# mLSTM scan: 20 thrown-away products of 512 columns at its opening are given up

## The chip, the cores and the metric

The kernel runs on one core of one Trainium2 chip. The metric is the device time of that core in microseconds (us), from launch to end. A core has TensorE for matrix products (PE in the profile, with its weight loads as a row of their own, PEld), VectorE (DVE), ScalarE (ACT), GpSimd (POOL) and SyncE (SP); they run beside one another and wait for one another through semaphores.

## The reference

Two layers of a diffusion backbone work on 1024 latent tokens and 256 context tokens of width 1024. Each layer projects its tokens once and hands the columns to four mixers: differential attention, a bidirectional mLSTM, a bidirectional gated linear attention (GLA) and windowed attention. A gate, one output projection and a residual follow. The part that bears on the change is the mLSTM, run forward and backward over the tokens in chunks, with a state (`cmat`, `nvec`, `m`) that is carried from chunk to chunk:

```
def _mlstm_step(state, xs):
    cmat, nvec, m = state
    q, k, v, li, lf = xs
    b = jnp.cumsum(lf, axis=-1)
    d = jnp.where(tril, b[..., :, None] - b[..., None, :] + li[..., None, :], -jnp.inf)
    m_t = jnp.maximum(m_inter, jnp.max(d, axis=-1))
    w = jnp.exp(d - m_t[..., None])
    s = jnp.einsum('bhtd,bhsd->bhts', q, k) * w
    num = jnp.einsum('bhts,bhsv->bhtv', s, v) + g_inter[..., None] * jnp.einsum('bhvd,bhtd->bhtv', cmat, q)
    nq = jnp.sum(s, axis=-1) + g_inter * jnp.einsum('bhd,bhtd->bht', nvec, q)
    h = num / jnp.maximum(jnp.abs(nq), jnp.exp(-m_t))[..., None]
    cmat = decay[..., None, None] * cmat + jnp.einsum('bhs,bhsv,bhsd->bhvd', w_end, v, k)
```

## The kernel before, in words

The program is a row of stages, run for each of the two layers; a stage is a block in which every engine has its own instruction list, and the engines meet at the end of a block. In `stage_mlstm` a first block (line 845) projects the tokens, convolves and gates them, turns them (line 949) and prepares decays. The second block (line 1128) is the scan, and it is the one the change touches. The GLA stage, whose block opens at line 1460, comes right behind it.

The scan works on chunks of 128 tokens: 10 chunks by two directions, 20 units in the list `UNITS`, forward and backward in turn. For one unit TensorE issues five groups, four heads each:

- `logs(u)`: the exponents of the weights, as one product of 128x512 that lays down the mask (line 1207, from the tiles `same`, an identity, and `neg`, the mask) and four of 128x128 that add the rows of gate sums (line 1210, from `row_parts` and `sel`). It writes PSUM bank `u % 2`.
- `scores(u)`: q times k of the four heads (line 1218).
- the new state's share, keys by scaled values (line 1238), and the share of the old state (line 1241).
- the weighted scores by the values (line 1248).

TensorE runs ahead by one unit: its list is logs(0), scores(0), and then for each u: logs(u+1), lines 1238 and 1241 of u, scores(u+1), line 1248 of u. ScalarE takes the exponential of each head's logs (line 1258). VectorE multiplies it with the scores (`weigh`, line 1277) and combines the parts into state and result (`finish`, lines 1285 to 1301). GpSimd divides and scales the values (lines 1173 to 1187).

At the opening, GpSimd copies `neg` and `same` (lines 1166 and 1167, signal `parts`), and VectorE copies and splits the gate sums into `row_parts` and copies `sel` (lines 1263, 1264 and 1267, signal `lows`, three increments). `logs(0)` waits for both signals. Ahead of it TensorE's list holds a loop of `WARM = 20` products of 128x512 on `same` and `neg` (lines 1222 to 1225), which waits for `parts` alone and writes PSUM bank 1. Nothing reads what it writes there; logs(1) later writes that bank anew.

Of the kernel before, what the change touches and what calls it, by code (L numbers as in the profile page):

```python
# [23 lines left out]
P = 128  # L24
# [9 lines left out]
HEADS = 4  # L34
# [69 lines left out]
def layer_program(nc, dram):  # L104

    ctx = ExitStack()
    with ctx:
# [37 lines left out]
        for layer in range(DEPTH):  # L145
            env["layer"], env["last"] = layer, layer == DEPTH - 1
            for stage in (stage_entry, stage_mlstm, stage_gla, stage_diff_attention,
                          stage_window_attention, stage_gates, stage_output):
                with ExitStack() as own:
                    stage_ctx.append(own)  # L150
                    stage(nc, env)

                    nc.all_engine_barrier(sems_to_clear=range(first_free, first_free + len(stage_sems)))
                    if stage is stage_output:
                        nc.all_engine_barrier(sems_to_clear=range(loaded[0].sem.num, slab_used.sem.num + 1))
                stage_sems.clear()
# [653 lines left out]
def stage_mlstm(nc, env):  # L810
    ps, signal, yT, ring = (env[n] for n in ("ps", "signal", "yT", "ring"))
    outer = ExitStack()
    with outer:
# [31 lines left out]
        with ExitStack() as own, nc.Block() as block:  # L845
# [8 lines left out]
            @block.sync  # L854
            def _(sp):
                for n in range(2 * PARTS):
                    i, ks = n // PARTS, slice(n % PARTS * KT // PARTS, (n % PARTS + 1) * KT // PARTS)
                    proj.wait_used(sp, n)
                    at = SLAB_AT[S_MG + i]
                    src = env["dram"]["w"][env["layer"] * P:(env["layer"] + 1) * P, at + ks.start * 512:at + ks.stop * 512]  # L860
                    sp.dma_start(mod_w[:, i, ks, :].rearrange("p k n -> p (k n)"), src).then_inc(env["loaded"][S_MG + i].sem, 16)
                def move_rows():
                    sp.wait_ge(v_ones.sem, 4)
                    sp.wait_ge(lanes_ready.sem, 1)
                    for way in range(2):
                        for t in range(NT):
                            sp.dma_start(row_b[32 * way:32 * way + HEADS, t * P:(t + 1) * P],
                                         g_cm[64 * way + HEADS * t:64 * way + HEADS * (t + 1), :]).then_inc(row_moved.sem, 16)

                proj.release(sp, 1)  # L870
                for part in range(PARTS):
                    proj.wait_used(sp, 2 * KT + 2 * part)
                    load_part(sp, env, S_CV, part)
                move_rows()
                proj.release(sp, 3)
                load_slabs(sp, env, S_CQK, S_CQK + 1)
                sp.wait_ge(row_moved.sem, 2 * NT * 16)
# [250 lines left out]
        with ExitStack() as own, nc.Block() as block:  # L1128
            def tile(name, shape, dt=F32):
                return own.enter_context(env["sbuf"](name, shape, dt))  # L1130
# [3 lines left out]
            neg = tile("b_neg", [P, 2, P], F32R)  # L1134
            same = tile("b_same", [P, P], F32R)
# [5 lines left out]
            num = tile("b_num", [P, 2, HEADS, DH + 1])  # L1141
            den = tile("b_den", [P, 2, HEADS])
            NU = len(UNITS)
            WARM = 20

            def col(j, q, way):
                return cols[:, q, 64 * way + HEADS * j:64 * way + HEADS * (j + 1)]
# [1 line left out]
            def span(u):  # L1149
                return slice(UNITS[u][2] * P, (UNITS[u][2] + 1) * P)  # L1150

            def half(h):
                return slice(64 * (h % 2), 64 * (h % 2) + 64)

            def fresh_of(u, hp=slice(0, 2)):
                return ps[:, 4 + 2 * (u % 2), 2 * (DH + 1):4 * (DH + 1)].rearrange("p (a d) -> p a d", a=2)[:, hp, :]

            def intra_of(u):
                return ps[:, 5 + 2 * (u % 2), 2 * (DH + 1):6 * (DH + 1)].rearrange("p (h d) -> p h d", h=HEADS)

            def inter_of(u):
                return ps[:, 4 + 2 * (u % 2):6 + 2 * (u % 2), 0:2 * (DH + 1)].rearrange("p o (e d) -> p e o d", e=2)
# [34 lines left out]
            @block.tensor  # L1197
            def _(pe):
                def logs(u):
                    way, i, j = UNITS[u]  # L1200
                    if u == 0:
                        pe.wait_ge(parts.sem, 2)
                        pe.wait_ge(lows.sem, 3)
                    if u >= 2:
                        pe.wait_ge(w_ready.sem, HEADS * (u - 1))
                    bank = ps[:, u % 2, :]
                    pe.matmul(bank.rearrange("p (h t) -> p h t", h=HEADS), same[:, :],
                              neg[:, way, :].unsqueeze(1).broadcast_to([P, HEADS, P]), start=True, stop=False, skip_group_check=True)
                    for h in range(HEADS):
                        last = pe.matmul(bank[:, h * P:(h + 1) * P], sel[:, way * HEADS + h, :], row_parts[:, span(u)],  # L1210
                                         start=False, stop=h == HEADS - 1, skip_group_check=True)
                    last.then_inc(d_mm.sem, 1)

                def scores(u):
                    if u >= 1:
                        pe.wait_ge(sw_ready.sem, u)
                    for h in range(HEADS):
                        last = pe.matmul(ps[:, 2 + h % 2, h // 2 * P:(h // 2 + 1) * P], qkT[half(h), 2 + h // 2, span(u)],
                                         qkT[half(h), h // 2, span(u)], start=True, stop=True, tile_position=(64 * (h % 2), 0))
                    last.then_inc(s_mm.sem, 1)  # L1220

                pe.wait_ge(parts.sem, 2)
                for i in range(WARM):
                    pe.matmul(ps[:, 1, :].rearrange("p (h t) -> p h t", h=HEADS), same[:, :],
                              neg[:, 0, :].unsqueeze(1).broadcast_to([P, HEADS, P]), start=True, stop=True)
                logs(0)
                scores(0)
                for u, (way, i, j) in enumerate(UNITS):
                    if u + 1 < NU:
                        logs(u + 1)  # L1230
                    if u == 0:
                        pe.wait_ge(zeroed.sem, 1)
                    if u >= 2:
                        pe.wait_ge(state_ready.sem, 2 * (u - 1))
                        pe.wait_ge(num_ready.sem, u - 1)
                    pe.wait_ge(vw_ready.sem, u + 1)
                    for h in range(HEADS):
                        last = pe.matmul(fresh_of(u)[half(h), h // 2, :], ktm[:, j, h * DH:(h + 1) * DH],
                                         vw[:, u % 2, h, :], start=True, stop=True)
                    for h in range(HEADS):  # L1240
                        last = pe.matmul(inter_of(u)[:, h // 2, h % 2, :], qkT[half(h), h // 2, span(u)],
                                         state[half(h), way, h // 2, :], start=True, stop=True, tile_position=(64 * (h % 2), 0))
                    last.then_inc(u_mm.sem, 1)
                    if u + 1 < NU:
                        scores(u + 1)
                    pe.wait_ge(sw_ready.sem, u + 1)
                    for h in range(HEADS):
                        last = pe.matmul(intra_of(u)[:, h, :], sw[:, h, :], v1[:, j, h, :], start=True, stop=True)
                    last.then_inc(intra_mm.sem, 1)
# [186 lines left out]
def stage_gla(nc, env):  # L1436
# [3 lines left out]
    with outer:  # L1440
# [19 lines left out]
        with ExitStack() as own, nc.Block() as block:  # L1460
# [4 lines left out]
            BANKS = 6  # L1465
            WARM = 8
            NP = NT // 2
# [29 lines left out]
            def _(pe):  # L1497
# [51 lines left out]
                pe.wait_ge(first_decays.sem, 1)  # L1549
                for _ in range(WARM):  # L1550
                    pe.matmul(ps[:, 0, :], la_hi[:, 0, 0:P], la_hi[:, 0:2, :].rearrange("p t c -> p (t c)"), start=True, stop=True)
# [1438 lines left out]
```

## Time and profile before

| | us |
|---|---|
| median of 3 runs | 2335.21 |
| lowest and highest run | 2332.82 and 2339.88 |
| the profiled execution | 2340.97 |
| its span, first to last instruction | 2339.2 |
| PE busy in the span | 1982.7 (85%) |
| mean granted clock of TensorE | 0.929 |

[...] Times in the trace count from the first instruction. A matmul's own duration is longer than the distance to the next one, since they are pipelined; how fast TensorE works is read from the distance between starts. In a row of the timeline the bracket at the end tells how long the engine had been idle and who released it.

### The profile page before, as it was taken

The page shows a single profiled execution, that of the slowest core. Times are in us where ns is not written, and L with a number is a line of the kernel's source. Part 1 is how long each engine was busy: PE and PEld are TensorE (multiplying, and loading weights), DVE is VectorE, ACT ScalarE, POOL GpSimd, SP SyncE. Part 2 cuts the span into 40 slices and gives each one's busy share as a digit, 9 for nine tenths or more (in the row PEclk, how much of TensorE's full clock was granted, in tenths as well). Part 3 has the DMA queues.
Part 4 walks back from the last instruction along what each step waited for, and adds up shares of the span by engine and source line. Part 5 has one row for each costly group of instructions (what it writes and reads, how often), then busy time and mean ns, then how long its engine had stood idle before and what let it go on. Part 6 is the DMA issues. An engine that isn't in the chain of part 4 may idle for free. (4 is left out here: it accounts for less than half of the span.)

```text
span 2339.2 us, 37578 instructions
## 1 busy us (share of the span) xinstructions
PE 1982.7 (85%) x14664; PEld 1644.9 (70%) x14664; DVE 1354.3 (58%) x2545; ACT 985.9 (42%) x2076; POOL 500.5 (21%) x642
## 2 busy tenths in 40 slices
PE   5889889897777868898987988988987778688988
PEld 3778778786665647787866877877876566577767
DVE  5156428778878367222765356268578782672257
ACT  5243332336868436311224333322358684262121
POOL 2203325311010100322214124244120101002212
PEclk8899999998989979999998999998989898799999
DMA  9840350240000410313239601600420004102231
GB/s 397 294 139 2 96 158 2 58 124 1 1 1 1 140 41 1 91 58 125 113 124 337 197 27 46 182 27 5 116 62 1 1 1 131 49 2 72 72 127 54
DMA packets 69614, 203.25 MB, mean 87 GB/s; under 512 B 8096, under 2 KB 11456, under 8 KB 65984
## 3 DMA queue, kind: packets, MB, share of 16 engines
q0 software_dynamic: 38016, 93.34, 14.0%
q1 hardware_dynamic: 26240, 98.08, 11.6%
q10 hardware_dynamic: 5184, 9.44, 1.1%
q8 instruction: 118, 1.93, 0.3%
q14 instruction: 56, 0.46, 0.1%
HBM read 180.83 MB, written 19.92 MB: 86 GB/s over the span
## 5 line engine op out<-in xcount | busy, mean ns | idle before, releaser
L774 PE MATMUL ps<-ring_lo,h_hi 128*128 128x512 f32 (+3 forms) x800 | 271.5, 340 | 0.0
L774 PE MATMUL ps<-h_hi,ring_lo 128*128 128x512 f32 (+1 forms) x688 | 251.0, 365 | 0.0
L2375 DVE TENSOR_REDUCE a_st<-ps 128x1 f32<-128x1280 f32 (+1 forms) x144 | 196.7, 1369 | 42.7 <-PE ps L2260 42.2
L2328 ACT ACTIVATE ring<-ps,a_st 128x1280 f32<-128x1280 f32 (+1 forms) x144 | 177.4, 1232 | 54.7 <-DVE a_st L2375 54.4
L2260 PE MATMUL ps<-a_k,a_q 128*128 128x512 f32 (+1 forms) x400 | 126.7, 427 | 53.1 <-ACT ring L2328 48.7
L774 PEld LDWEIGHTS ps<-ring_lo,h_hi 128*128 128x128 f32 x800 | 158.7, 198 | 13.6 <-issue 0.5
L774 PE MATMUL ps<-h_hi,g_proj_wh 128*128 128x512 f32 (+1 forms) x400 | 148.9, 372 | 12.1 <-DVE ring_lo L732 7.2
L774 PE MATMUL ps<-g_proj_xl,g_proj_wh 128*128 128x512 f32 (+1 forms) x400 | 148.3, 371 | 0.0
L774 PEld LDWEIGHTS ps<-h_hi,ring_lo 128*128 128x128 f32 x688 | 130.3, 189 | 21.3
L2277 PE MATMUL ps<-cst,ring 128*128 128x128 f32 x656 | 107.2, 296 | 42.2 <-ACT ring L2337 16.3
L2260 PEld LDWEIGHTS ps<-a_k,a_q 128*128 128x128 f32 x400 | 73.8, 213 | 82.0 <-ACT ring L2328 65.7
L2753 PE MATMUL ps<-o_w_hi,o_y_hi 128*128 128x512 f32 x288 | 113.8, 395 | 17.1 <-DVE o_y_lo L2788 8.8
L2277 PEld LDWEIGHTS ps<-cst,ring 128*128 128x128 f32 x656 | 79.6, 150 | 63.9 <-ACT ring L2337 20.7
L774 PE MATMUL ps<-a_proj_wh,h_hi 128*128 128x512 f32 (+1 forms) x320 | 111.6, 349 | 7.0 <-DVE ring_lo L732 7.0
L2754 PE MATMUL ps<-o_w_lo,o_y_hi 128*128 128x512 f32 x288 | 113.3, 393 | 0.0
L2755 PE MATMUL ps<-o_w_hi,o_y_lo 128*128 128x512 f32 x288 | 113.3, 393 | 0.0
L2816 ACT ACTIVATE o_y_hi<-yT 128x640 fp32r<-128x640 f32 (+1 forms) x64 | 43.5, 686 | 152.7 <-PE ps L2755 144.3
L774 PE MATMUL ps<-a_proj_wh,a_proj_xl 128*128 128x512 f32 (+1 forms) x320 | 104.7, 336 | 0.0
L2665 DVE TENSOR_TENSOR par<-ps,par 128x512 f32<-128x512 f32 (+1 forms) x40 | 25.3, 636 | 136.9 <-ACT par L2647 136.9
L2647 ACT ACTIVATE par<-ps 128x512 f32<-128x512 f32 (+1 forms) x50 | 27.7, 554 | 180.7 <-PE ps L774 159.0
L2395 DVE SCALAR_TENSOR_TENSOR ring<-ring,a_st 128x1280 f32<-128x1280 f32 (+1 forms) x72 | 102.6, 1425 | 0.1
L2682 POOL TENSOR_TENSOR yT<-yT,par 128x512 f32<-128x512 f32 (+1 forms) x50 | 61.2, 1238 | 179.2 <-DVE par L2665 153.5
(379 smaller groups left out, 5258.5 us busy)
## 6 DMA issues: line engine op xcount, KB each, us to landing
ring<-in_w SPq DMA_DIRECT2D x14, 2048.0 KB, 7.5
a_proj_xl<-h_low POOLq DMA_DIRECT2D x64, 320.0 KB, 3.2
ring<-in_w SPq DMA_DIRECT2D x32, 512.0 KB, 3.8
b_proj_xl<-h_low POOLq DMA_DIRECT2D x22, 640.0 KB, 4.4
d_proj_xl<-h_low POOLq DMA_DIRECT2D x32, 320.0 KB, 3.2
h_low<-h_low SPq DMA_DIRECT2D x32, 256.0 KB, 4.1
yT<-in_w SPq DMA_DIRECT2D x16, 512.0 KB, 7.2
g_proj_xl<-h_low POOLq DMA_DIRECT2D x32, 256.0 KB, 5.5
```

What stands on the lines that cost most here:

```text
L774: last = pe.matmul(out, left, right, start=k == 0 and (p, q) == self.HIGH[0], stop=k == KT - 1 and (p, q) == self.LOW[0])
L2260: last = pe.matmul(ps[:, 3 * c + b, 0:w], q4[:, 2 * h + c, t * P:(t + 1) * P], k4[:, 2 * h + c, k0:k0 + w], start=True, stop=True)
L2277: last = pe.transpose(ps[:, 6 + n % 2, (k - a) * P:(k - a + 1) * P], p(u, 0, T)[:, k * P:(k + 1) * P], C(env, "ident"))
L2328: act.activation(p(u, c, n), ps[:, 3 * c:3 * c + 3, :].rearrange("p b n -> p (b n)")[:, 0:n], ACT.Exp, bias=st[:, 0:1], accum_out=st[:, 1: ...
L2375: dve.tensor_reduce(stat[:, u % SLOTS, c, 0:1], ps[:, 3 * c:3 * c + 3, :].rearrange("p b n -> p (b n)")[:, 0:n], AX.X, ALU.max, negate=Tru ...
L2395: dve.scalar_tensor_tensor(out=p(u, 0, n), in0=p(u, 1, n), scalar=st[:, 0, 3:4], in1=p(u, 0, n), op0=ALU.mult, op1=ALU.add).then_inc(comb. ...
L2647: act.activation(sig[:, n % 2, 0:w], ps[:, n % 8, 0:w], ACT.Sigmoid).then_inc(sg.sem, 1)
L2682: pool.tensor_tensor(y, y, sig[:, n % 2, 0:b[1]], ALU.mult).then_inc(done.sem, 1)
L2753: pe.matmul(ps[:, n % 8, :], y_hi[:, at, tile], w_hi[:, at, :], start=k == 0, stop=False)
L2754: pe.matmul(ps[:, n % 8, :], y_hi[:, at, tile], w_lo[:, at, :], start=False, stop=False)
L2755: last = pe.matmul(ps[:, n % 8, :], y_lo[:, at, tile], w_hi[:, at, :], start=False, stop=k == KT - 1)
L2816: act.activation(y_hi[:, i % BUFS, 0:HT], yT[:, k, toks(half)], ACT.Copy).then_inc(split_hi.sem, 1)
```

## The change

The loop of 20 products and its own wait for `parts` go out of TensorE's list, and with them the constant. `logs(0)` keeps both of its waits. Nothing else is touched. The lines behind move up by one, and those behind the loop by five.

```diff
@@ -1141,7 +1141,6 @@
             den = tile("b_den", [P, 2, HEADS])
             NU = len(UNITS)
-            WARM = 20
 
             def col(j, q, way):
@@ -1219,10 +1218,6 @@
                     last.then_inc(s_mm.sem, 1)
 
-                pe.wait_ge(parts.sem, 2)
-                for i in range(WARM):
-                    pe.matmul(ps[:, 1, :].rearrange("p (h t) -> p h t", h=HEADS), same[:, :],
-                              neg[:, 0, :].unsqueeze(1).broadcast_to([P, HEADS, P]), start=True, stop=True)
                 logs(0)
                 scores(0)
```

TensorE's list at the opening of the scan's block, before (`b_neg` and `b_same` are the tiles `neg` and `same`, `xN` stands for N in a row):

```order
536 L845 UNCONDITIONAL_BRANCH
537 L1197 UNCONDITIONAL_BRANCH
538 L1224 MATMUL ps<-b_neg,b_same 128x512 x20
539 L1207 MATMUL ps<-b_neg,b_same 128x512
540 L1210 MATMUL ps<-b_row_parts,b_sel 128x128 x4
541 L1218 MATMUL ps<-b_qkT 128x128 x4
542 L1207 MATMUL ps<-b_neg,b_same 128x512
```

The same place on TensorE with the change:

```order
536 L845 UNCONDITIONAL_BRANCH
537 L1196 UNCONDITIONAL_BRANCH
538 L1206 MATMUL ps<-b_neg,b_same 128x512
539 L1209 MATMUL ps<-b_row_parts,b_sel 128x128 x4
540 L1217 MATMUL ps<-b_qkT 128x128 x4
541 L1206 MATMUL ps<-b_neg,b_same 128x512
```

The group of 20 is gone, and logs(0) is the first thing TensorE does in the block. The order of all that follows is the same, in both layers, and so are the lists of the other engines.

## Rows read from the trace of the kernel before

**Rows 1.** The page: engines' busy time, and the granted clock in 40 slices.

```profile
PE 1982.7 (85%) x14664; PEld 1644.9 (70%) x14664; DVE 1354.3 (58%) x2545; ACT 985.9 (42%) x2076; POOL 500.5 (21%) x642
PEclk8899999998989979999998999998989898799999
```

**Rows 2.** Timeline, first layer's opening: start, us, engine, line, instruction, idle and releaser.

```profile
176.54 0.89 POOL L1167 CAST b_same<-cst 128x128 fp32r<-128x128 f32 x1
177.48 6.50 PE L1224 MATMUL ps<-b_neg,b_same 128*128 128x512 f32 x20 [5.68 <-POOL b_same L1167]
178.28 1.52 DVE L1267 TENSOR_TENSOR b_row_parts<-yT,b_row_parts 64x1280 fp32r<-64x1280 f32 x1
183.82 0.39 PE L1207 MATMUL ps<-b_neg,b_same 128*128 128x512 f32 x1
184.65 1.14 ACT L1258 ACTIVATE b_wgt<-ps,ring 128x128 f32<-128x128 f32 x4 [7.17 <-PE ps L1210]
185.88 0.76 DVE L1277 TENSOR_TENSOR b_sw<-ps,b_wgt 128x256 f32<-128x256 f32 x2 [6.09 <-ACT b_wgt L1258]
187.49 1.11 PE L1248 MATMUL ps<-b_v,b_sw 128*128 128x65 f32 x8
188.40 0.48 PE L1207 MATMUL ps<-b_neg,b_same 128*128 128x512 f32 x1
```

**Rows 3.** Timeline, second layer's opening, the same instructions.

```profile
1368.66 6.48 PE L1224 MATMUL ps<-b_neg,b_same 128*128 128x512 f32 x20 [5.76 <-POOL b_same L1167]
1369.46 1.51 DVE L1267 TENSOR_TENSOR b_row_parts<-yT,b_row_parts 64x1280 fp32r<-64x1280 f32 x1
1374.98 0.39 PE L1207 MATMUL ps<-b_neg,b_same 128*128 128x512 f32 x1
```

**Rows 4.** Stretches of the scan: length, busy of PE, PEld, DVE, ACT, POOL; PEclk, DMA share, GB/s.

```profile
170.75:177.57 6.82, 1.14 (x5) 0.74 (x5) 6.12 (x6) 3.52 (x4) 1.31 (x3) 0.50 0.00 0
177.57:180.99 3.42, 3.42 (x8) 2.72 (x9) 2.19 (x3) 0.00 (x0) 2.71 (x2) 0.50 0.00 0
180.99:184.40 3.41, 3.41 (x18) 2.79 (x16) 0.00 (x0) 0.00 (x0) 0.00 (x0) 1.00 0.00 0
184.40:252.66 68.26, 63.40 (x730) 56.81 (x730) 44.07 (x170) 22.80 (x80) 26.88 (x44) 1.00 0.01 2
1368.83:1372.24 3.41, 3.41 (x8) 2.65 (x9) 2.11 (x3) 0.00 (x0) 2.62 (x2) 0.50 0.02 5
```

**Rows 5.** Timeline of PE at a projection's opening, products of 512 columns.

```profile
446.12 0.80 PE L774 MATMUL ps<-a_proj_wh,h_hi 128*128 128x512 f32 x1 [3.50 <-DVE ring_lo L732]
450.12 0.63 PE L774 MATMUL ps<-ring_lo,h_hi 128*128 128x512 f32 x1
450.55 0.44 PE L774 MATMUL ps<-a_proj_wh,h_hi 128*128 128x512 f32 x1
451.06 0.40 PE L774 MATMUL ps<-a_proj_wh,h_hi 128*128 128x512 f32 x1
451.29 0.40 PE L774 MATMUL ps<-ring_lo,h_hi 128*128 128x512 f32 x1
```

**Rows 6.** Timeline of PE, one unit of the scan and the next one's start.

```profile
188.72 0.56 PE L1210 MATMUL ps<-b_row_parts,b_sel 128*128 128x128 f32 x4
190.68 1.10 PE L1248 MATMUL ps<-b_v,b_sw 128*128 128x65 f32 x8
191.59 0.48 PE L1207 MATMUL ps<-b_neg,b_same 128*128 128x512 f32 x1
```

**Rows 7.** Timeline, the scan's end and the next stage's start.

```profile
256.28 0.68 POOL L1185 TENSOR_TENSOR yT<-yT,b_num 128x256 f32<-128x256 f32 x1
258.07 1.78 ACT L724 ACTIVATE c_proj_wh<-ring 128x288 fp32r<-128x288 f32 x5 [9.38 <-PEq L153]
```

**Rows 8.** Stretches of the GLA scan's opening, of line 2170, and of GLA's last products.

```profile
341.41:361.89 20.48, 17.38 (x145) 12.79 (x144) 10.20 (x12) 6.01 (x9) 10.14 (x9) 0.50 0.03 13
655.44:658.85 3.41, 3.28 (x16) 3.31 (x17) 3.41 (x9) 3.02 (x8) 2.60 (x5) 0.50 0.01 2
1628.24:1632.41 4.17, 4.17 (x19) 3.90 (x18) 2.04 (x4) 0.00 (x0) 0.00 (x0) 0.50 0.00 0
```

## The prediction

> **What bounds the kernel now.** I read the page first, then the timeline of the scan's opening in both layers, then the stretches with their granted clock. On the page PE is busy for 85% of the span and its clock hardly ever stands at full in a whole slice [rows 1]: TensorE is the engine to follow, and what a microsecond of its work costs depends on its clock. Over the scan the two are tied. A unit takes 3.19 us (188.40 to 191.59, the start of line 1207 to the next one), and PE is busy for 63.40 of the 68.26 us from 184.40 on, at clock 1.00 [rows 2, 4, 6]. So PE paces the scan even at full clock, and the others wait for it.
>
> At the opening TensorE has been nearly idle (1.14 us busy of 6.82) and its clock is 0.50 [rows 4]. The 20 products start at 177.48, right behind GpSimd's copy of `same` (176.54 + 0.89 = 177.43), and hold TensorE until logs(0) starts at 183.82. What logs(0) itself needs is there much earlier: VectorE's last split of the gate sums ends at 178.28 + 1.52 = 179.80. ScalarE has then been idle for 7.17 us and VectorE for 6.09 when they get their first work [rows 2]. Nothing but the 20 products keeps logs(0) back. When the scan ends (256.28 + 0.68 = 256.96), the next stage's first instruction starts at 258.07, released by the meeting of the engines and by no transfer [rows 7]. So what the scan gains or loses is passed on whole.
>
> **The first term: the earlier start.** With the 20 products gone, logs(0) starts at 179.80 plus about 0.03 for the release, 179.83 in place of 183.82: 3.99 us. In the second layer VectorE ends at 1369.46 + 1.51 = 1370.97, so logs(0) starts at about 1371.00 in place of 1374.98: 3.98 us [rows 3]. Together 7.97 us. The 20 products took 6.34 us from first start to logs(0); 2.35 us of that lay beside VectorE's split and gives nothing back. What is late next at the opening is this split (line 1267). GpSimd's first scaled values are needed only by line 1238, two groups later, and hide behind logs(0) and scores(0).
>
> **The second term: the clock.** The 20 products do one thing for the scan: eight of them run at 0.50 until 180.99, and from then the clock is 1.00 and stays so for the whole scan, in which PE is never idle for long [rows 4]. In both layers it rose 3.5 us after the first product (177.48 to 180.99, 1368.66 to 1372.24) [rows 2 to 4]. A projection needed a little longer: first product at 446.12, at half pace until about 450.55 [rows 5]. With the 20 products gone the same climb has to be made by the scan's own work, and TensorE gets 2.35 us longer of idleness ahead of it, which changes nothing, as the clock is at its lower level already.
>
> What half clock costs is read from distances: products of 512 columns start 0.43 us apart at 0.50 (450.12 to 450.55) and 0.23 apart at 1.00 (451.06 to 451.29) [rows 5]. PE's groups of the scan would take about twice as long. From logs(0) to the second unit's line 1207 PE takes 4.58 us at full clock (183.82 to 188.40) [rows 2], and 9.2 us at half. In that opening the list runs on without a gap, as the answers of ScalarE (1.14 us) and VectorE (0.76 us) are hidden beside PE's slower groups. So the scan's first microseconds are about as dense as the projection's, and each microsecond at half clock does half a microsecond of the scan.
>
> How long will it last? The lower bound is the 3.5 us of the densest opening; the upper one, for work of small pieces, is the GLA scan's opening, which stays at 0.50 from 341.41 to 361.89, 20.5 us, with PE busy 17.38 of them [rows 8]. The mLSTM scan's opening is nearer to the projections: no waits, and 0.6 to 1 us of small products between those of 512 columns. I take 5 us. The loss is 5 x 0.5 = 2.5 us per layer, within 1.8 (3.5 us) and 10.2 (20.5 us). Below nothing it can't go, since no product runs faster at half clock; nothing at all would be lost if the opening waited for other engines, whose work is 1.14 + 0.76 us in the chain from the first logs to the first weighted scores.
>
> The sum: 3.99 - 2.5 = 1.5 us gained per layer, 3.0 in both. The profiled execution, 2340.97 us, would become 2338.0; against the median of the runs, which is 5.76 lower, 2335.21 - 3.0 = 2332.2. The break-even is a climb of 8 us: there the clock costs the 4 us that the start gives.
>
> [...] By my sum the scan itself makes the climb for 2.5 us, where the 20 products cost it 4.
>
> **Rivals.**
>
> A climb that takes long (slower). The place is the scan's first three to six units, the price half of each microsecond at 0.50, and it decides from 8 us of climb on. For it: the GLA scan's opening, and GLA's last products (lines 1778 and 1781), which keep PE busy for the whole of 4.17 us and leave the clock at 0.50; line 1781 has 64 columns, much like line 1248's 65 here [rows 8]. Against it: line 2170, of 128 columns and back to back, ended its 3.41 us at 0.50 with the clock up, and the scan keeps its clock for 68 us [rows 4, 8]. With 20.5 us in both layers: 2 x (10.2 - 3.99) = +12.5, 2347.7 us; in one layer alone, with my 1.5 gained in the other: +4.7, 2339.9.
>
> The clock never rises in the scan. All 20 units at half clock would add up to 20 x 3.19 = 63.8 us per layer, less the 3.99: +119.6, 2454.8 us. For it speaks only that the scan's products are small; against it, the same as above, and that a unit at half clock leaves PE no waits at all. [...]
>
> Nothing is lost. If the opening is bound by the chain logs, exponential, weighting and not by PE, or if the clock rises within 1 to 2 us of logs(0), nearly the whole 7.97 us stay: 2327.2 us. For it: the chain of the first unit is the only place where the three engines work in turn. Against it: line 1248 of the first unit starts at 187.49, 0.85 us after its weighted scores were there (185.88 + 0.76 = 186.64) [rows 2]; PE was the late one even at full clock.
>
> The change does nothing: something else holds logs(0) until 183.8. Nothing in the trace does. 2335.2 us.
>
> **How the numbers follow.** My forecast has 0.66, by itself from 2328.5 to 2337: the climb taken as 3.5 to 6.5 us gives 2330.8 to 2333.7, and the three runs of before lie 7 us apart, so that a median can be off by 2 to 3. The long climb has 0.15, the clock that never rises 0.03, nothing lost 0.13, no effect 0.03. The predicted time is the first one's, 2332.2. The range reaches down to 2326.5, which takes in nothing lost, and up to 2342, which takes in a long climb in one layer; both layers' long climb and the clock that never rises are left out. A measurement of this kernel tells about 0.3%, 7 us, from no change. Faster by more needs nearly all of the 7.97 us: half of that rival and a tenth of my own case, 0.13. Slower by more is the long climb in both layers or worse, with some of the runs' spread: 0.14. The rest, 0.73, is within 0.3%.
>
> **What would show it.** In the new trace logs(0) should start 0.03 us behind the end of VectorE's split, about 179.83, and in the second layer 4 us earlier relative to the block's start too. A row of 0.50 should reach 3.5 to 6.5 us into the scan; within it the products of 128x128 should start 0.2 us or more apart. The second unit's line 1207 should start 1 to 2 us earlier than 188.40, and from there on units of 3.19 us at clock 1.00. The next stage should start earlier by that much. I am wrong if the clock is still at 0.50 8 us into the scan, if it falls again within the scan, or if logs(0) does not move.

## The result and the profile after

| | us |
|---|---|
| before, median (lowest to highest) | 2337.22 (2332.82 to 2339.88), 4 runs |
| after, median (lowest to highest) | 2424.12 (2417.58 to 2440.69), 4 runs |
| ratio, 95% interval | 1.0382, 1.0353 to 1.0411 |
| profiled execution, before and after | 2340.97 and 2421.39 |

The change makes the kernel 87 us slower. It lies far outside the range that was forecast. One of the four runs of after has a trace. In the tables below, where the runs of a kernel lie in a faster and a slower group, the ratio is that of the faster group.

The page of the profile after, against [rows 1]: PE is busy for 84 us more, though 40 products fewer stand in the program. The fourth and fifth slices have a clock of 5 tenths, and the 24th to 26th, the second layer's scan, 6, 5 and 7, where before had 9 in all five. The clock is given as a share of TensorE's full speed; the traces have 0.50 and 1.00 alone, and a value between is the mean of a stretch that had both.

```profile
PE 2066.8 (85%) x14624; PEld 1723.9 (71%) x14624; DVE 1354.7 (56%) x2545; ACT 986.4 (41%) x2076; POOL 498.6 (21%) x642
PEclk8895598999989979999998965789998999899999
```

The timeline of the first layer's opening, where [rows 2] has it before. The block starts 1.46 us later in this execution (ScalarE's table load at 177.65, at 176.19 in before), so times are compared from there. Line 1206 is line 1207 of before, 1262 is 1267, 1243 is 1248.

```profile
177.65 1.28 ACT L1253 ACT_TABLE_LOAD   x1 [1.19 <-PEq L845]
179.74 1.51 DVE L1262 TENSOR_TENSOR b_row_parts<-yT,b_row_parts 64x1280 fp32r<-64x1280 f32 x1
181.40 0.77 PE L1206 MATMUL ps<-b_neg,b_same 128*128 128x512 f32 x1 [8.58 <-DVE b_row_parts L1262]
184.00 0.79 PE L1206 MATMUL ps<-b_neg,b_same 128*128 128x512 f32 x1
188.11 1.97 PE L1243 MATMUL ps<-b_v,b_sw 128*128 128x65 f32 x8
189.83 0.77 PE L1206 MATMUL ps<-b_neg,b_same 128*128 128x512 f32 x1
195.65 0.77 PE L1206 MATMUL ps<-b_neg,b_same 128*128 128x512 f32 x1
```

logs(0) starts 3.75 us into the block, where it was 7.63: the earlier start is there, 3.88 us of it. But the next units stand 5.82 us apart (189.83 to 195.65), not 3.19 [rows 2, 6].

Stretches of after, with the columns of [rows 4]: the scan from logs(0) on, the next projection's first products, and what follows.

```profile
181.39:299.00 117.61, 117.03 (x740) 105.39 (x740) 45.22 (x175) 22.86 (x80) 28.51 (x47) 0.50 0.00 1
304.00:309.38 5.38, 5.38 (x23) 5.38 (x24) 5.22 (x12) 5.36 (x11) 3.66 (x6) 0.50 0.99 275
309.38:320.00 10.62, 9.90 (x58) 7.75 (x58) 5.86 (x10) 2.94 (x6) 1.86 (x4) 1.00 0.50 138
```

The clock never rises in the scan. PE is busy for 117.03 of 117.61 us, with as many products as before and the same 22.8 us of ScalarE's work; only TensorE is slow, at 0.50 from end to end. The clock comes up 5.5 us after the next projection's first product (303.91), where [rows 5] had 4.4. The stage is measured from the block's start, ScalarE's table load, to the next stage's first instruction, in the row that answers to [rows 7]. Before, the start in the first layer, then start and end in the second:

```profile
176.19 1.28 ACT L1258 ACT_TABLE_LOAD   x1 [1.19 <-PEq L845]
1367.37 1.28 ACT L1258 ACT_TABLE_LOAD   x1 [1.21 <-PEq L845]
1449.23 1.77 ACT L724 ACTIVATE c_proj_wh<-ring 128x288 fp32r<-128x288 f32 x5 [9.38 <-PEq L153]
```

After, the end in the first layer (its start is in the timeline above), then start and end in the second:

```profile
302.85 1.44 ACT L724 ACTIVATE c_proj_wh<-ring 128x288 fp32r<-128x288 f32 x4 [11.37 <-PEq L153]
1410.44 1.28 ACT L1253 ACT_TABLE_LOAD   x1 [1.20 <-PEq L845]
1535.65 1.77 ACT L724 ACTIVATE c_proj_wh<-ring 128x288 fp32r<-128x288 f32 x5 [11.38 <-PEq L153]
```

That is 125.20 us where before had 81.88 (176.19 to 258.07): +43.3 us. The second layer has the same difference, 125.21 against 81.86. Twice 43.3 is 86.7 us, and the medians lie 86.9 apart. The two profiled executions differ by 80.4 only: up to the end of the second scan's stage it is 86.4, and what follows took 6 us less in the execution of after.

### The profile page after: what moved, and what is told of

Its sections match the earlier page's. It is cut to its first block and busy times, and to the rows that moved or that the text cites. A ratio compares the mean times of both kernels' runs of the same rounds, so it can differ in the third digit from the quotient of the medians.

```text
span 2419.6 us, 37498 instructions
## 1 busy us (share of the span) xinstructions
PE 2066.8 (85%) x14624; PEld 1723.9 (71%) x14624; DVE 1354.7 (56%) x2545; ACT 986.4 (41%) x2076; POOL 498.6 (21%) x642
## 5 line engine op out<-in xcount | busy, mean ns | idle before, releaser
L2748 PE MATMUL ps<-o_w_hi,o_y_hi 128*128 128x512 f32 x288 | 114.0, 396 | 17.1 <-DVE o_y_lo L2783 8.8
L1253 ACT ACTIVATE b_wgt<-ps,ring 128x128 f32<-128x128 f32 x160 | 45.7, 368 | 179.4 <-PE ps L1209 179.4
L1272 DVE TENSOR_TENSOR b_sw<-ps,b_wgt 128x256 f32<-128x256 f32 x80 | 30.3, 419 | 138.8 <-PE ps L1243 132.9
```

What stands on the lines that cost most here:

```text
L1253: act.activation(wgt[:, u % 2, h, :], ps[:, u % 2, h * P:(h + 1) * P], ACT.Exp, bias=col(j, 0, way)[:, h:h + 1])\
L1272: ins = dve.tensor_tensor(sw[:, o::2, :], ps[:, 2 + o, 0:2 * P].rearrange("p (e t) -> p e t", e=2), wgt[:, u % 2, o::2, :], ALU.mult)
L2748: pe.matmul(ps[:, n % 8, :], y_hi[:, at, tile], w_hi[:, at, :], start=k == 0, stop=False)
```

## The experiments

The experiments were measured in five groups, each beside runs of the kernel before, whose medians were 2330.9 (one run; e1 to e4), 2338.6 (23 runs), 2337.5 (17), 2335.3 (one run; e8 and e9) and 2338.5 us (18; the last experiment).

**A burst in the middle.** Of the kernel after, with the 20 products ahead of the seventh unit:

```diff
                 for u, (way, i, j) in enumerate(UNITS):
+                    if u == 6:
+                        pe.wait_ge(w_ready.sem, HEADS * u)
+                        for _ in range(20):
+                            pe.matmul(ps[:, 1, :].rearrange("p (h t) -> p h t", h=HEADS), same[:, :], ...)
```

> No products at the opening; the 20 products of 512 columns stand ahead of the seventh unit (u = 6). Theory A (the scan can hold the full clock but its own products are too thin to raise it): units 0 to 5 take 5.8 us each at 0.50, the clock rises 3.5 to 7 us into the 20 products and stays at 1.00 to the scan's end, units of 3.2 us. Per layer 6 or 7 slow units (+2.6 us each) and 6 to 7 us of burst, less the 4 us of the earlier start: about +19, so near 2375 us. Theory B (it is the opening that decides: the longer idleness ahead of logs(0), or where in its cycle the clock was caught): the burst in the middle raises the clock for a few microseconds at most and it falls back, about 2430 us.

Measured: 2377.31 us, with 2330.94 for before beside it. The timeline of PE at the burst, and the stretches ahead of it, in it and behind it:

```profile
217.65 6.42 PE L1227 MATMUL ps<-b_neg,b_same 128*128 128x512 f32 x20
223.91 0.39 PE L1206 MATMUL ps<-b_neg,b_same 128*128 128x512 f32 x1
227.01 0.48 PE L1206 MATMUL ps<-b_neg,b_same 128*128 128x512 f32 x1
```

```profile
180.00:217.60 37.60, 37.49 (x235) 33.71 (x236) 12.34 (x47) 7.98 (x28) 7.75 (x13) 0.50 0.00 1
217.65:221.00 3.35, 3.35 (x10) 2.67 (x10) 2.32 (x9) 0.00 (x0) 0.41 (x1) 0.50 0.00 0
221.00:272.20 51.20, 47.00 (x518) 41.86 (x517) 30.54 (x119) 14.83 (x52) 19.73 (x33) 1.00 0.01 1
```

37.6 us of the scan's own work, with PE busy for all but 0.1 us of it, leave the clock at 0.50. The burst raises it 3.4 us after its first product, and the same scan holds 1.00 for the 51 us that are left. The second layer does the same: the clock rises in the burst (first product at 1434.26, clock up at 1436.2) and holds to the scan's end. So it is not the opening's place or its idleness that counts (theory B falls): the scan can keep the clock and, in the 37.6 us here and the 117 us of after, doesn't raise it.

The 3.5 to 7 us that this and later expectations give the climb are my estimate: the lower end is the 3.5 us of [rows 2 to 4], and no run shows the 7. Where a burst raised the clock in the traces, it was 1.9 (e1, second layer) to 5.2 us (e8, first layer) after its first product. Of a cycle of the clock the traces show this much: within each of them its changes lie whole multiples of 3.41 us apart, in before at 170.75, 180.99, 256.08 and 262.91 (10.24, 75.09 and 6.83 us: 3, 22 and 2 times), in e1 at 169.85, 221.05, 272.25 and 282.49 (15, 15 and 3 times).

**Denser units.** No burst; 4, then 2, more products of 512 columns at the head of each unit's logs, whose result is overwritten:

```diff
                     bank = ps[:, u % 2, :]
+                    for _ in range(4):
+                        pe.matmul(bank.rearrange("p (h t) -> p h t", h=HEADS), same[:, :], ...)
```

> No burst at the opening; each unit's logs starts with 4 more products of 512 columns, whose result is overwritten. Theory A: the denser unit raises the clock by itself in the first two or three units (within 15 us); then a unit takes 3.2 + 4 x 0.23 = 4.1 us. Per layer +20 x 0.92 = 18.4, a climb of some 4, less 4: about 2335 + 2 x 18.5 = 2372 us. Theory B: the clock stays at 0.50, units of 5.82 + 4 x 0.43 = 7.5 us, about 2424 + 2 x 34 = 2492 us.

> No burst at the opening; each unit's logs starts with 2 more products of 512 columns. With 4 more the clock rose 3.2 us after the first logs in one layer, and some 20 us after it in the other. If two are enough, the clock rises within some 40 us and a unit then takes 3.2 + 2 x 0.23 = 3.65 us: per layer +20 x 0.46 = 9.2, a climb of 5 to 20, less 4: 2350 to 2385 us. If not, 0.50 throughout with units of 5.82 + 2 x 0.43 = 6.7 us: 2424 + 2 x 17 = 2458 us.

Measured: 2367.41 us with 4 more, 2405.26 with 2, one run each. With 4, the scan raised the clock by itself in both layers, 3.2 us after its first product in the first layer (180.78 to 184.0) and 15.9 us after it in the second (1383.35 to 1399.2); the stretches of the first:

```profile
180.78:184.00 3.22, 3.22 (x11) 2.62 (x11) 0.00 (x0) 0.00 (x0) 0.33 (x1) 0.50 0.00 0
184.00:265.90 81.90, 81.12 (x811) 71.49 (x811) 44.82 (x174) 22.87 (x80) 27.14 (x45) 1.00 0.01 2
```

With 2, it did in the second layer and not in the first, so that the time lies between the two that were expected:

```profile
181.00:300.00 119.00, 118.34 (x681) 104.66 (x682) 39.37 (x151) 20.53 (x72) 24.10 (x39) 0.50 0.00 1
1443.50:1515.20 71.70, 70.67 (x761) 63.07 (x761) 44.07 (x171) 21.66 (x76) 27.09 (x45) 1.00 0.01 2
```

More work made it faster than after: the 160 additional products save 57 us. PE's row reads busy nearly all the time in each of these (81.12 of 81.90 us, 118.34 of 119.00), and in the scan's own units too (117.03 of 117.61), which never raised the clock.

**Bursts of other shapes.** In place of the 20 products at the opening, each back to back, with 40 weight loads. The 8.5 us at half clock of the expectations are 40 times 0.21 us, the distance at 0.50 in the trace of before: of line 1781's eight records of 64 columns the last six take 1.28 us (1628.78 to 1630.06), and line 2170's of 128 columns start 0.21 us apart at 0.50 too (655.81 to 656.02). The first group of line 1781 and the start of what follows it, in the stretch at 0.50 of [rows 8]:

```profile
1628.46 1.81 PE L1781 MATMUL ps<-yT,ring 128*128 128x64 f32 x8
1630.06 1.17 PE L1778 MATMUL ps<-c_state,yT 128*128 128x256 f32 x2
```

Its 1.60 us at 0.50 do not show by themselves that 64 columns are too thin; the bursts of e2 and e7 test it. The diff shows the bodies of the six runs one below the other; each run has one of them, and e3 has 128 where e2 has 64:

```diff
-                for i in range(WARM):
-                    pe.matmul(ps[:, 1, :].rearrange("p (h t) -> p h t", h=HEADS), same[:, :], ...)
+                for i in range(40):     # e2, e3: the mask on the identity, fp32r, 64 and 128 columns
+                    pe.matmul(ps[:, 1, 0:64], same[:, :], neg[:, 0, 0:64], start=True, stop=True)
+                    # e5: turns, full fp32
+                    pe.transpose(ps[:, 1, 0:P], qkT[:, 2, 0:P], C(env, "ident"))
+                    # e6: kept tokens, fp32r, 128 columns
+                    pe.matmul(ps[:, 1, 0:P], env["h_hi"][:, 0, 0:P], env["h_hi"][:, 0, 0:P], ...)
+                for i in range(20):     # e7, e8: keys, full fp32 (two passes each), 64 and 128 columns
+                    pe.matmul(ps[:, 1, 0:DH], qkT[:, 2, 0:P], qkT[:, 3, 0:DH], ...)
```

> In place of the 20 products of 512 columns, 40 of 64 columns on the same weights stand at the opening, with 128 rows, back to back, about 8.5 us at half clock. Theory A: 64 columns per weight load are too thin, as line 1781 in the trace of before; the clock stays at 0.50 through the burst and the scan, about 2424 + 2 x 4.5 = 2433 us. Rival C (any back-to-back work of PE without a wait raises the clock, and the scan failed for its short waits between groups): the clock rises within 3.5 to 7 us, time near before's, 2335 to 2339 us.

> The same with 40 products of 128 columns and 128 rows. By line 2170 in the trace of before, which raised the clock, theory A says that this shape suffices: the clock rises 3.5 to 7 us after the first one and the scan holds 1.00, logs(0) near 184, time near before's 2335 us (within 3). If only long products (512 columns) raise it, the clock stays at 0.50: about 2433 us.

> In place of the 20 products, 40 turns of 128 columns of the real keys against the identity, in full fp32, as line 2170 has them; back to back they take 8.5 us at half clock. The burst of 40 products of 128 columns on mask and identity did not raise the clock. Theory D (what counts is the data and the number format: line 2170's real fp32 data raised it): the clock rises 3.5 to 7 us after the first turn and the scan holds 1.00, about 2333 us. Theory E (the shape of 128 columns is too thin for a clock that has been low for a while, whatever the data): 0.50 to the scan's end, about 2436 us.

> 40 products of 128 columns at the opening, in fp32r as the mask's, but on the kept tokens (dense real numbers) as both operands. The 40 on identity and mask left the clock at 0.50, 40 fp32 turns of real keys raised it. Theory D1 (the data decide, a weight tile of real numbers against an identity): the clock rises within 3.5 to 7 us, about 2333 to 2340 us. Theory D2 (the number format decides, full fp32 against fp32r): 0.50 through the scan, about 2436 us.

> At the opening 20 full fp32 products of 64 columns on real keys (each is two passes, so 40 weight loads and 40 passes of 64 columns), the shape of the scan's line 1248. If the narrowness of the scan's products is what keeps the clock down, as line 1781 in the trace of before suggests, it stays at 0.50 through burst and scan, about 2433 us; if real fp32 data suffice at any width, the clock rises 3.5 to 7 us after the first one, about 2335 us.

> 20 full fp32 products (not turns) of 128 columns on real keys at the opening: 40 weight loads and 40 passes of 128 columns, back to back. If full fp32 at 128 columns is what raises the clock, it rises 3.5 to 7 us after the first one and the scan holds it, about 2332 to 2339 us. If the turn as such made the difference, the clock stays at 0.50 through burst and scan, about 2437 to 2445 us.

| burst | format, operands | us | clock |
|---|---|---|---|
| e2, 64 columns | fp32r, mask on identity | 2436.29 | 0.50 through burst and scan |
| e3, 128 columns | fp32r, mask on identity | 2436.49 | 0.50 through burst and scan |
| e6, 128 columns | fp32r, real tokens | 2436.93 | 0.50 through burst and scan |
| e7, 64 columns | full fp32, real keys | 2444.98 | 0.50 through burst and scan |
| e5, 128 columns, turns | full fp32, real keys | 2332.22 | up 3.9 us after the first |
| e8, 128 columns | full fp32, real keys | 2336.83 | up 5.2 us after the first |

The bursts of e2 and e3 with the logs(0) behind them, 8.55 and 8.59 us from first product to logs(0):

```profile
178.87 8.74 PE L1224 MATMUL ps<-b_neg,b_same 128*128 128x64 f32 x40 [5.67 <-POOL b_same L1167]
187.42 0.77 PE L1207 MATMUL ps<-b_neg,b_same 128*128 128x512 f32 x1
```

```profile
177.67 8.79 PE L1224 MATMUL ps<-b_neg,b_same 128*128 128x128 f32 x40 [5.67 <-POOL b_same L1167]
186.26 0.73 PE L1207 MATMUL ps<-b_neg,b_same 128*128 128x512 f32 x1
```

The stretches of the bursts of e6, e7 and e8, and the scan behind e8:

```profile
177.60:186.00 8.40, 8.40 (x40) 8.40 (x41) 2.09 (x3) 0.00 (x0) 2.60 (x2) 0.50 0.00 0
```

```profile
177.70:186.00 8.30, 8.30 (x40) 8.30 (x40) 2.19 (x3) 0.00 (x0) 2.70 (x2) 0.50 0.00 0
```

```profile
178.80:183.90 5.10, 5.10 (x24) 5.10 (x25) 2.21 (x3) 0.00 (x0) 2.73 (x2) 0.50 0.00 0
183.90:255.00 71.10, 66.21 (x755) 59.61 (x755) 44.40 (x171) 22.81 (x80) 26.89 (x44) 1.00 0.01 2
```

In all three PE and PEld are busy for the whole stretch and each record of a matmul starts 0.21 us behind the one before (a full fp32 product has two records: the 20 of e7 stand as x40). In this row they can't be told apart, and yet one raises the clock and two don't. Real data don't do it (e6 against e3), nor full fp32 at 64 columns (e7); full fp32 at 128 columns does, as a turn or as a product (e5, e8), and fp32r does at 512 columns (up 3.5 us after the first in before). My expectation of e3 was wrong; e6 and e7 each decided between two theories. All of the table is single runs, but each has two layers that agree, and the two outcomes lie 100 us apart. Two things are not separated: e8 differs from e6 in its data (keys, not tokens) as well as in its format, and full fp32 on mask and identity was not run.

The scan's unit is made in the main of such products: 65 columns on 128 rows (lines 1238 and 1248, near e7) and fp32r of 128 columns (1210, as e3). With them stand products on 64 rows (1218, 1241), which no burst tried, and one of 512 columns. That the unit fails because of these shapes fits the bursts and the denser units; which of its groups weighs how much is not shown.

**How many of the 20 are needed.**

```diff
-            WARM = 20
+            WARM = 4
```

(and 8, and 14)

> 4 products in place of 20, 1.7 us at half clock, all of it beside VectorE's split, so that the scan starts as early as without any. With 8 nearly every layer found the full clock. If the climb adds the burst and the scan's own first 512-column products up, 4 will do in some layers: times in groups near 2329, 2372 and 2415 us. If a burst must be dense over its whole climb by itself, 4 give nothing: all near 2416 us.

> 8 products in place of 20: as many as ran at half clock in the trace of before, 3.5 us. If the climb is a matter of how long the dense stretch lasts and where it falls, 8 are at the edge: in some layers the clock rises near the end of the burst (then 2 to 3 us faster than with 20 per layer), in others it stays at 0.50 through the scan (+41 us for that layer). So the times should fall into groups: about 2331, 2374 and 2417 us. If a count of products alone decides, all runs stand together, near 2331.

> 14 products, 6 us at half clock if none of them sees the full one. Theory A: enough in nearly every case; the scan starts 6 x 0.23 = 1.4 us earlier per layer than with 20, 2.8 us in both: ratio about 0.999. If the climb needs up to 7 us, one layer in five or so misses it (+41 us), and the times fall into two groups.

| WARM | runs, us | ratio (95%) |
|---|---|---|
| 0 | 2417.6 to 2440.7 (4) | 1.0382 (1.0353 to 1.0411) |
| 4 | 2415.0, 2417.7, 2419.3 | 1.0342 (1.0322 to 1.0362) |
| 8 | 2328.7 to 2341.7 (9), 2365.8 | 0.9980 (0.9962 to 0.9999) |
| 14 | 2330.9 to 2343.7 (6), 2351.2 to 2370.6 (4) | 1.0007 (0.9978 to 1.0035) |
| 20 | 2327.4 to 2354.2 (23) | 1 |

The ratio of 8 leaves out its run of 2365.8 us, that of 14 its two slowest (2368.9 and 2370.6). By their times four products give nothing and eight nearly always do. In the profile with 8 the clock was still at 0.50 when logs(0) started, and rose 1.2 us into it (burst at 177.64, clock up at 182.40):

```profile
177.64:182.40 4.76, 4.76 (x13) 3.93 (x13) 2.28 (x3) 0.00 (x0) 2.79 (x2) 0.50 0.00 0
182.40:254.00 71.60, 64.33 (x736) 57.58 (x736) 46.48 (x180) 22.80 (x80) 28.64 (x47) 1.00 0.01 2
```

So the burst need not last until the clock is up. Whether the scan's first products helped to raise it, or it would have risen then in any case, is not shown.

The same trace has something else. In the second layer the clock was up at 1366.8 us and fell again at 1431.6, 7 us before the scan's last product ended. A row of PE's timeline, and the stretches on both sides of the fall:

```profile
1431.07 0.45 PE L1238 MATMUL ps<-b_vw,yT 128*64 128x65 f32 x8 [0.91 <-POOL b_vw L1173]
1423.00:1431.60 8.60, 7.00 (x84) 6.31 (x86) 5.95 (x24) 3.30 (x12) 4.30 (x7) 1.00 0.01 3
1431.60:1448.70 17.10, 11.61 (x66) 10.84 (x67) 9.19 (x30) 5.38 (x13) 8.86 (x14) 0.50 0.24 69
```

It cost little: this stage took 81.99 us where the first layer's took 79.66, and the run, 2328.7 us, is the fastest of the ten.

14 was meant to be safer than 8 and was not, within what ten runs tell; why is open, as none of its four runs above 2350 us has a trace.

**Dense work where TensorE waits anyway.** The first try puts 9 products at the end of the block before and 9 at the scan's opening, which wait for nothing; the second, the bridge, fills nearly all of TensorE's waits from the turns to logs(0):

```diff
+                    if n in (2, 4):                      # bridge alone: ahead of turns 3 and 5
+                        pe.wait_ge(proj.read.sem, proj.first[-1])
+                        for _ in range(6):
+                            pe.matmul(ps[:, 0, :], env["h_hi"][:, 0, 0:P], env["h_hi"][:, 0, 0:512], ...)
...
+                pe.wait_ge(proj.read.sem, proj.first[-1])
+                for _ in range(9):                       # bridge: 16; behind the last turn
+                    pe.matmul(ps[:, 0, :], env["h_hi"][:, 0, 0:P], env["h_hi"][:, 0, 0:512], ...)
...
-                pe.wait_ge(parts.sem, 2)
-                for i in range(WARM):
+                for _ in range(9):                       # bridge: 15; opening of the scan
+                    pe.matmul(ps[:, 1, :], env["h_hi"][:, 0, 0:P], env["h_hi"][:, 0, 0:512], ...)
```

> The dense work moved to where TensorE waits anyway: 9 products of 512 columns on the kept tokens (h_hi) at the end of the block before, behind the last turn (line 949), and 9 at the opening of the scan's block, which wait for nothing. The clock should be up before VectorE's split of the gate sums is done, logs(0) should start 0.03 to 0.3 us behind that split (about 3.8 us earlier than in before, in both layers), and the scan should hold 1.00: 7 to 8 us faster, ratio about 0.997. Rival: the 0.5 us of the meeting between the blocks breaks the dense stretch, or the burst delays the meeting; then the clock is up late, or the gain is only 2 to 4 us.

> The clock is not let fall at all: TensorE is kept busy with thrown-away products of 512 columns on the kept tokens through its waits, 6 ahead of the turns 3 and 5 (line 949), 16 behind the last turn, 15 at the opening of the scan's block, while logs(0) waits for VectorE's split as without a burst. The burst of 9 and 9 left 2.8 and 1.4 us of idleness and the clock fell 1.8 us into the scan. If idleness ahead of the scan is what lets it fall, PEclk is 1.00 from the projection through the scan in both layers, logs(0) starts within 0.3 us of the split's end, and the gain is the whole first term, 7 to 8 us: ratio 0.9966 (0.995 to 0.998). Rival: the products delay the turns or the meeting of the engines, and 1 to 3 us of it are lost per layer: ratio 0.998 to 1.000.

The first try: 2340.9, 2367.9 to 2374.1 (4 runs) and 2417.9 us; ratio 1.0113 (1.0069 to 1.0156), with the last left out. Only the run of 2417.9 us has a trace, and in it both layers went without the clock (the stages took 123.77 and 123.56 us). That the four runs in the middle lost it in one layer is a guess from the times, and the steps, 30 and 47 us, are not alike. The timeline of PE and the stretches:

```profile
172.16 2.31 PE L953 MATMUL ps<-h_hi 128*128 128x512 f32 x9
177.28 2.33 PE L1225 MATMUL ps<-h_hi 128*128 128x512 f32 x9 [2.81 <-PEq L845]
180.99 0.47 PE L1209 MATMUL ps<-b_neg,b_same 128*128 128x512 f32 x1 [1.39 <-DVE b_row_parts L1267]
```

```profile
172.10:182.75 10.65, 6.46 (x35) 4.79 (x34) 8.01 (x8) 4.38 (x8) 4.02 (x4) 1.00 0.00 0
182.80:296.00 113.20, 113.20 (x726) 102.25 (x724) 44.80 (x173) 21.97 (x77) 27.28 (x45) 0.50 0.00 1
```

The clock was at full when logs(0) started. With 2.81 and 1.39 us of idleness behind it, it fell 1.8 us into the scan, and the scan never got it back. So a burst that ends too early can be lost.

The bridge reaches up to logs(0) (its last product starts right ahead of it), with 1.21 us of idleness left where the engines meet: 1.00 from the projection to the scan's end in the first layer, and the stage takes 78.07 us, 3.8 less than before. Ten of its twelve runs lie between 2326.9 and 2343.2 us, two at 2363.8 and 2368.9; median 2330.98, ratio 0.9978 (0.9960 to 0.9996), the two left out. In its second layer the clock fell at 1431.5, some 10 us before the scan's end. PE's timeline there:

```profile
1429.38 0.56 PE L1216 MATMUL ps<-b_row_parts,b_sel 128*128 128x128 f32 x4
1430.85 0.45 PE L1242 MATMUL ps<-b_vw,yT 128*64 128x65 f32 x8 [0.91 <-POOL b_vw L1179]
1431.23 0.94 PE L1245 MATMUL ps<-b_state,b_qkT 64*128 64x65 f32 x8
```

PE had waited 0.91 us for GpSimd's scaled values just before, in the same unit as in the trace with 8 products. But that wait alone does not decide it: the second layers of before, e1, e5, e8 and WARM = 14 have it too, 0.91 or 0.92 us long, and kept the clock. As with 8 products the fall cost little (this stage took 80.68 us), and this run, 2331.64 us, is among the ten.

**Without PE's waits for the scaled values.** GpSimd scales the values of unit u + 2 before it divides unit u:

```diff
                 for u in range(NU):
-                    divide(u)
                     if u + 2 < NU:
                         scale_v(u + 2)
+                    divide(u)
```

> The kernel before with its 20 products, and GpSimd scales the values of unit u + 2 before it divides unit u, not behind. PE's waits of up to 0.9 us for b_vw should be gone (1.4 and 2.3 us in all per layer in before). Theory: they cost 2 to 4 us in both layers and are what lets the clock fall within the scan in some runs; so 2 to 5 us faster (ratio 0.998 to 0.999) and a narrower spread than before's 2327 to 2354 us. Rival: the division is late now and VectorE's next combination waits for it, or the state (DVE L1289) ends the wait instead: ratio 1.000 and the same spread.

> The bridge and GpSimd's new order together. The bridge alone had 10 of 12 runs between 2326.9 and 2343.2 us, 2 at 2364 and 2369. If PE's waits for b_vw are what lets the clock fall inside the scan, the two groups become one and the median is 2 to 4 us below the bridge's, near 2327 us (ratio 0.995 to 0.997). If not, the spread stays and the ratio is the bridge's 0.998.

| kernel | runs, us | median | ratio (95%) |
|---|---|---|---|
| before | 2327.7 to 2351.0 (18) | 2338.53 | 1 |
| new order alone | 2323.5 to 2337.5 (12) | 2330.03 | 0.9964 (0.9942 to 0.9986) |
| bridge and new order | 2313.6 to 2333.3 (7) | 2321.48 | 0.9923 (0.9890 to 0.9955) |

What PE waited for within the scan, in before (184 to 252 us); with the new order no row is left between 184 and 249 us:

```profile
PE ps L1238 <- DVE b_state L1289: 3.4, 4, 0.9
PE ps L1238 <- POOL b_vw L1173: 1.4, 6, 0.6
```

Those are 4.8 us per layer, and the stage is 5.0 us shorter in the first layer (175.83 to 252.74, 76.91 against 81.88) and 4.5 in the second (77.39). I had expected 2 to 5 us in all; measured are 8.5, since the waits that the rows put down to VectorE's state are gone as well. With the bridge too it is 73.04 (175.90 to 248.94) and 73.02, 8.8 us shorter in each layer: the 4.8 of the waits and 4 of the earlier start. Twice 8.8 is 17.7, measured 17.1. The bridge with the new order:

```profile
179.66 0.47 PE L1213 MATMUL ps<-b_neg,b_same 128*128 128x512 f32 x1
248.94 1.77 ACT L724 ACTIVATE c_proj_wh<-ring 128x288 fp32r<-128x288 f32 x5 [8.33 <-PEq L153]
```

```profile
165.00:180.00 15.00, 13.20 (x66) 9.96 (x65) 13.38 (x14) 8.31 (x11) 4.03 (x4) 1.00 0.21 70
180.00:246.00 66.00, 64.00 (x740) 57.64 (x738) 46.20 (x178) 22.81 (x80) 28.24 (x46) 1.00 0.01 2
```

This is the fastest kernel of the study, 17 us faster than before. None of the 19 runs with the new order lay apart from the others. That is weak evidence that the waits had cost those two runs the clock: only 7 of the 19 have the bridge, and if two of twelve lie apart, seven in a row without one come about in 28 of 100 cases. The two traces with a fall inside the scan have it so late that it cost 2 to 3 us, while the bridge's runs of 2363.8 and 2368.9 us lie 33 and 38 us above its median; at 2.63 us lost per unit (5.82 against 3.19), that is 12 units and more at half clock. What happened in those runs is open. What is shown is the 8.8 us per layer.

## Why the prediction was wrong

- **What bounds the kernel.** Right. PE paces the scan, nothing but the 20 products held logs(0) back, and the change of the scan's length went on whole to the next stage.
- **The first term.** Right: logs(0) 3.88 us earlier from the block's start, where 3.99 was forecast; 0.15 us instead of 0.03 went by behind VectorE's split.
- **The second term, where it failed.** The step reads: "the scan's first microseconds are about as dense as the projection's, and each microsecond at half clock does half a microsecond of the scan", and from it a climb of 5 us. The second half held roughly (5.82 us for a unit where 3.19 was). The first did not: I read density from PE's busy time and from the lack of waits, and took the small products between two of 512 columns for 0.6 to 1 us. The rows say otherwise: a unit of 3.19 us has one product of 512 columns, of 0.32 us, and 2.87 us of small ones (188.40, 188.72, 191.59 in [rows 2, 6]). The scan is busy at half clock for 117.03 of 117.61 us and doesn't raise the clock; e6, e7 and e8 have the same busy row and different ends. Being busy did not decide; what the products were made of did. The 20 products of 512 columns raised the clock at the opening and in the middle, and 4 more of them in each unit did in both layers.
- **The bounds.** The climb was bounded by 20.5 us, from GLA's opening [rows 8]. There the clock rose within other work, at 361.89 us; a scan that can't raise it at all has no such bound, and that the clock held for 68 us [rows 4] says nothing on it, since holding and raising are two things. The row that pointed the right way was GLA's last products, 4.17 us with PE busy throughout, line 1781 with 64 columns among them (0.21 us from record to record), at 0.50 [rows 8]; alone it was too short to settle it, as the projection's products of 512 columns needed 4.4 us [rows 5]. I named it and set line 2170 against it. Line 2170 is full fp32 with 128 columns and 128 rows, like e8, and the scan has no such group.
- **The rival with 0.03** was the one that came true. Its price, +119.6 us, was too high, for two reasons. It doubled the 3.19 us, but PE's groups took 1.66 to 1.89 times as long, 1.82 for the unit (5.82 us), and the unit had no waits at full clock. And 20 x (5.82 - 3.19) = 52.6 us less the 3.9 of the start would be 48.7 per layer; the 4.8 us for which PE waited in before were gone in after, which leaves 43.9, where 43.3 was measured.
- **What the 20 products paid for.** By my sum the scan makes the climb by itself for 2.5 us, where the 20 products cost it 4. The runs show that it does not make it, and that just any products ahead of it don't either: e2, e3, e6 and e7 are 8.5 to 8.6 us of them and left the clock at 0.50. The 20 paid 4 us per layer for something that the scan did not get in 117 us.

## What to carry to other kernels

Ask two questions of a stretch, not one: does its work hold TensorE's full clock, and can it raise it? A loop of small products (64 columns, 64 rows, fp32r of 128) held 1.00 for 70 us and stayed at 0.50 for 117 us, with PE busy in both; products that look like waste in front of it, 20 of 512 columns for 6.3 us, were worth 43 us. Here the best place for such work was where TensorE waits anyway, up to the first real product (78.07 us for the first layer's stage, against 81.88); taking away the waits inside the loop came on top (73.04 us).

## What the runs showed of the hardware that was not expected

- Back-to-back products of 128 columns on 128 rows raised the clock in full fp32 (up after 3.9 and 5.2 us) and did not in fp32r (8.6 us at 0.50, then the whole scan), with the same distance of 0.21 us between starts at half clock. The data were other ones too.
- A busy share of 100% of PE and PEld for 8.4 us (e6), or of over 99% of PE for 117 us (after), left the clock at 0.50. The page's row cannot show whether work raises it; the granted clock has to be read beside it.
- Four products of 512 columns ahead of the scan did nothing in three runs; with eight, nine of ten runs were as fast as with 20. In the one that was traced both layers got the full clock, and the second lost it again 7 us before the scan's last product ended.
- A wait of PE of 0.9 us stood just ahead of a fall of the clock inside the scan in two traces (the bridge and WARM = 8, second layers) and was followed by none in five others (before, e1, e5, e8, WARM = 14).
